# Seven products in place of eight for pairs of feed-forward column blocks, in a long float32 transformer kernel

## The reference

```
def swiglu(h, w_in, w_out):
    g, u = split_cols(h @ w_in, (D_FF, D_FF))        # D_FF = 2816
    return (jax.nn.silu(g) * u) @ w_out
x = x + 0.5 * swiglu(rms_norm(x, g), w_in[layer], w_out[layer])
```

## Time and profile before

| | |
|---|---|
| median of three runs | 1626.42 us (1625.85 to 1631.29) |
| profiled execution | 1626.7 us as the span from its first to its last instruction; the page gives no other time for it |
| PE busy | 1600.1 us (98%), 8058 matmuls |
| DVE busy | 1106.4 us (68%) |
| ACT busy | 862.0 us (53%) |
| POOL busy | 227.5 us (14%) |
| mean granted TensorE clock | 0.997 of full |

### The profile page before, as it was taken

One profiled execution on the slowest core, in us unless ns is written; L12 is line 12 of the kernel. 1 busy time (PEld: TensorE's weight loads), 2 busy tenths in 40 slices (PEclk: granted clock), 3 DMA queues, 4 the chain that ended last, 5 costly groups with the idle time before them and its releaser, 6 DMA issues.

```text
span 1626.7 us, 21211 instructions
## 1 busy us (share of the span) xinstructions
PE 1600.1 (98%) x8058; PEld 1337.7 (82%) x8058; DVE 1106.4 (68%) x1761; ACT 862.0 (53%) x1324; POOL 227.5 (14%) x351
## 2 busy tenths in 40 slices
PE   8999999999999999999999999999999999999998
PEld 6888877788888888888889888888889877888886
DVE  6775788867655556555596776655568997776566
ACT  5554556855545445444555555544454457454444
POOL 2499901000000000000000000000014442100000
PEclk9999999999999999999999999999999999999999
DMA  9766656445466565656655453565675554556653
GB/s 277 237 209 218 209 157 192 157 142 156 133 191 187 188 184 178 193 182 193 208 174 156 151 181 116 182 186 189 191 262 164 166 157 137 187 193 190 188 188 109
DMA packets 187543, 295.22 MB, mean 181 GB/s; under 512 B 13510, under 2 KB 108144, under 8 KB 186160
## 3 DMA queue, kind: packets, MB, share of 16 engines
q1 hardware_dynamic: 183264, 275.93, 54.6%
q0 software_dynamic: 3888, 17.60, 3.4%
q10 hardware_dynamic: 288, 0.33, 0.1%
HBM read 288.29 MB, written 5.25 MB: 180 GB/s over the span
## 4 chain that ended last, share of the span: by engine, by line
PE 86%; DVE 7%; ACT 3%; issue 2%; POOL 1%; DMA 0%; SPq 0%; DVEq 0%; ACTq 0%
PE b L445 25%; PE b L447 24%; PE b L446 24%; PE b L646 4%; DVE wlo L1655 2%; PE b L648 2%; ACT whi L1100 1%; PE b L669 1%; PE b L511 1%; PE b L899 1%; PE b L881 1%; PE b L608 1%; PE b L561 1%; PE b L527 1%; ACT R L1189 1%
## 5 line engine op out<-in xcount | busy, mean ns | idle before, releaser
L1655 DVE TENSOR_TENSOR wlo<-raw,whi 128x1024 fp32r<-128x1024 f32 (+1 forms) x523 | 648.5, 1243 | 436.5 <-ACT whi L1100 435.2
L1100 ACT ACTIVATE whi<-raw 128x1024 fp32r<-128x1024 f32 (+1 forms) x523 | 550.0, 1053 | 557.8 <-PE b L447 522.3
L445 PE MATMUL b<-whi,hT 128*128 128x512 f32 (+1 forms) x1040 | 413.4, 397 | 10.5 <-DVE wlo L1655 8.9
L447 PE MATMUL b<-whi,hT 128*128 128x512 f32 (+1 forms) x1040 | 405.1, 390 | 0.0
L446 PE MATMUL b<-wlo,hT 128*128 128x512 f32 (+1 forms) x1040 | 404.6, 389 | 0.0
L445 PE MATMUL b<-whi,oT 128*128 128x512 f32 x672 | 265.0, 394 | 0.0
L447 PE MATMUL b<-whi,oT 128*128 128x512 f32 x672 | 262.0, 390 | 0.0
L446 PE MATMUL b<-wlo,oT 128*128 128x512 f32 x672 | 261.6, 389 | 0.0
L445 PEld LDWEIGHTS b<-whi,hT 128*128 128x128 f32 x1040 | 196.1, 189 | 55.2 <-DVE wlo L1655 10.3
L447 PEld LDWEIGHTS b<-whi,hT 128*128 128x128 f32 x1040 | 196.0, 188 | 41.6
L446 PEld LDWEIGHTS b<-wlo,hT 128*128 128x128 f32 x1040 | 196.5, 189 | 37.9
(11 more groups left out here) (343 smaller groups left out, 1864.0 us busy)
## 6 DMA issues: line engine op xcount, KB each, us to landing
raw<-in_ffn_w_in SPq DMA_DIRECT2D x350, 256.0 KB, 3.2
raw<-in_ffn_w_out SPq DMA_DIRECT2D x88, 512.0 KB, 3.3
raw<-in_w_ff SPq DMA_DIRECT2D x64, 512.0 KB, 4.1
raw<-in_w_in SPq DMA_DIRECT2D x36, 512.0 KB, 3.7
raw<-in_x_w_kv SPq DMA_DIRECT2D x32, 512.0 KB, 4.1
raw<-in_even_w_in SPq DMA_DIRECT2D x24, 512.0 KB, 3.9
raw<-in_odd_w_in SPq DMA_DIRECT2D x24, 512.0 KB, 3.8
raw<-in_x_w_q SPq DMA_DIRECT2D x16, 512.0 KB, 4.0
```

What stands on the lines that cost most here:

```text
L445: T.matmul(out, ah, bh, start=start, stop=False, skip_group_check=skip)
L447: return T.matmul(out, al, bh, start=False, stop=stop, skip_group_check=skip)
L1100: E.activation(K.whi[j % NSPLIT][:, 0:n], K.raw[j % NRAW][:, 0:n], ACT.Copy).then_inc(*S.whi.done(j))
L1655: V.tensor_tensor(K.wlo[j % NSPLIT][:, 0:n], K.raw[j % NRAW][:, 0:n], K.whi[j % NSPLIT][:, 0:n].bitcast(F32), ALU.subtract).then_inc(*S.wl ...
```

## The change

For chunk pairs (2, 3), (4, 5) and (6, 7) of feed-forwards f1, f2 and f3, the product of h (256 x 1024) with a 1024 x 1024 part of `w_in` (512 gate and 512 up columns) is cut 2 x 2 and done with seven products of 128 x 512 by 512 x 512 in place of eight (`block`). Each product has two pieces of six matmuls each. A pair is called a block below, by its first chunk.

The seven need sums of the operands. POOL adds the sums of rows of h once for each feed-forward (2 operations of 128 x 1024 and 4 of 128 x 512) and makes four sums of weight tiles, T1 to T4, in two halves each, eight operations of 128 x 1024 for each block (`block_sums`). ACT and DVE split the sums as they split loaded tiles, so a block has 14 splits where two chunks had 8. Four partial results are joined on DVE out of PSUM and one copied by ACT; silus and multiplications are 128 x 512 now.

A block's eight tiles are loaded whole into buffers of their own (`tile_load`), 12 to 5 pieces ahead in SP's queue. These loads wait for POOL's sums that read the buffer before, in front of the ring's loads. The two or four rows of the chunks before come between the products: in block 2 behind P7 and P3, in blocks 4 and 6 behind P5, P2, P7 and P3. Chunk 8 has the four rows of chunks 6 and 7. The splits of the memory for layer 2 (`mem_halves(1, k)` and its low parts) move from chunks 5 and 6 of f1 to chunks 9 and 10 of f2.

```
+        self.tile = [R1[:, 1024 * i:1024 * i + 1024] for i in range(8)]
+        self.tsum = [R2[:, 1024 * i:1024 * i + 1024] for i in range(4)]
         self.vsb = sb("vsb", [P, 2, 512])
+        turned_heads = sb("sqj", [P, 1024])
+        self.tile += [self.vsb[:, :, :].rearrange("p a n -> p (a n)"), turned_heads[:, :]]
...
+    def factor(self, name, kt):
+        if name in ("P1", "P2", "P4"):
+            k, t = kt + 4 * (name != "P1"), int(name == "P4")
+            return tuple(a[:, k, P * t:P * t + P] for a in self.hT)
+        at = 512 * ("P5", "P6", "P7", "P3").index(name) + P * kt
+        return tuple(a[:, :, :].rearrange("p k t -> p (k t)")[:, at:at + P] for a in self.mT)
...
+    def ahead_of(self, c):
+        return [] if c == 0 else [c - 2, c - 1] if c - 2 in self.blocks else [c - 1]
 def downs(f, c):
     last = f.nch - 1
     if f.gated and c >= last - 1:
-        return [(last - 2, [c - last + 1])]
-    return [(c - 1, list(range(f.per)))] if 0 < c < last else []
+        more = [p for p in f.ahead_of(c) if p < last - 2] if c == last - 1 else []
+        return [(p, list(range(f.per))) for p in more] + [(last - 2, [c - last + 1])]
+    return [(p, list(range(f.per))) for p in f.ahead_of(c)] if c < last else []
+PRODUCTS = (("P1", 4, 1, "B11"), ("P6", 5, 1, "T2"), ("P5", 6, 1, "T1"), ("P2", 4, 0, "B21"), ("P7", 5, 0, "T3"),
+            ("P3", 6, 0, "B22"), ("P4", 5, 0, "T4"))
+TILES = {"B11": 0, "B12": 2, "B22": 4, "B21": 6}
+TSUMS = {"T1": 0, "T2": 2, "T3": 0, "T4": 2}
+TILE_LEAD = 12
...
-    Ffn("f1", 32, 0, "ffn2_w_in", "ffn2_w_out", 2816, True, 0.5, "x0"),
-    Ffn("f2", 40, 1, "ffn1_w_in", "ffn1_w_out", 2816, True, 0.5, "f1"),
-    Ffn("f3", 72, 1, "ffn2_w_in", "ffn2_w_out", 2816, True, 0.5, "x1"),
+    Ffn("f1", 32, 0, "ffn2_w_in", "ffn2_w_out", 2816, True, 0.5, "x0", (2, 4, 6)),
+    Ffn("f2", 40, 1, "ffn1_w_in", "ffn1_w_out", 2816, True, 0.5, "f1", (2, 4, 6)),
+    Ffn("f3", 72, 1, "ffn2_w_in", "ffn2_w_out", 2816, True, 0.5, "x1", (2, 4, 6)),
...
+            key, b, last_row = (f.name, c), f"{f.name}b{c}", [(p, kk) for p in f.ahead_of(c) for kk in range(f.per)]
+            shares = [0] * 7
+            for i in range(len(last_row)):
+                shares[5 - i % 4 if len(last_row) > 2 else 5 - i] += 1
+            for q, (name, bank, opens, of) in enumerate(PRODUCTS):
+                if name == "P2":
+                    pe.wait_ge(*S.snapped.at(key))
+                elif name == "P7":
+                    pe.wait_ge(*S.joined.at((*key, "U2")))
+                elif name == "P3":
+                    pe.wait_ge(*S.joined.at((*key, "V")))
+                elif name == "P4":
+                    pe.wait_ge(*S.joined.at((*key, "G1")))
+                else:
+                    open_bank(bank)
+                if name == "P6":
+                    pe.wait_ge(*S.slo.at((f.name, 1)))
+                for h in range(2):
+                    j = len(K.plan)
+                    K.at[b, 2 * q + h] = j
+                    kind = "tile" if of[0] == "B" else "sum"
+                    K.source.append((kind, key, f.slot(c, TILES[of] + h) if kind == "tile" else TSUMS[of] + h))
+                    K.plan.append((of, h, 0, 2, ((0, 512),)))
+                    pe.wait_ge(*S.wlo.at(j))
+                    hi, lo = K.split_views(j)
+                    for kk in range(2):
+                        ins = products(banks[bank][:, :], K.factor(name, 2 * h + kk), (hi[:, kk, :], lo[:, kk, :]),
+                                       bool(opens) and h == kk == 0, h == kk == 1, True)
+                    ins.then_inc(*S.dense.done(("w", j), *([(*key, name)] if h else [])))
+                    if q == 0 and h < len(f.ahead_of(c)):
+                        turn(f.ahead_of(c)[h])
+                for _ in range(shares[q]):
+                    p, kk = last_row.pop(0)
+                    down(p, [kk])
+            free[4] = (S.product.at((f.name, c, 0)),)
+            free[5] = (S.joined.at((*key, "U1")),)
+            free[6] = (S.joined.at((*key, "G0")),)
...
+            kind, of, i = K.source[j]
+            if kind == "ring":
+                act.wait_ge(*S.loaded[of % NRAW].at(j))
+            elif kind == "tile":
+                act.wait_ge(*S.tiled[i].at(of))
+            else:
+                act.wait_ge(*S.summed_w.at((*of, K.plan[j][0], K.plan[j][1])))
...
+            for o, p in enumerate(f.ahead_of(c)):
+                behind(o)
+                high(p)
+            behind(1)
+            act.wait_ge(*S.dense.at((*key, "P1")))
+            act.wait_ge(*S.product.at((f.name, c - 1, 1)))
+            E.activation(K.fs[0], banks[4][:, :], ACT.Copy).then_inc(*S.snapped.done(key))
+            behind(9)
+            opened(1, "G1")
+            behind(11)
+            opened(0, "G0")
+            weights(K.at[b, 13] + AHEAD)
...
+        def row_sums(i):
+            at = slice(1024 * i, 1024 * i + 1024)
+            act.wait_ge(*S.summed_w.at((f.name, "S", i)))
+            E.activation(K.mT[0][:, :, :].rearrange("p k t -> p (k t)")[:, at], K.R2[:, 2048 + 1024 * i:3072 + 1024 * i],
+                         ACT.Copy).then_inc(*S.shi.done((f.name, i)))
...
-    ffn(FFNS[1], {(5 + k // 4, k % 4): mem_halves(1, k) for k in range(8)}, {}, "f2", 40)
-    ffn(FFNS[2])
+    ffn(FFNS[1], {}, {}, "f2", 40)
+    ffn(FFNS[2], {(9 + k // 4, k % 4): mem_halves(1, k) for k in range(8)})
...
+            def joined(name, product, bank, first, out):
+                dve.wait_ge(*S.dense.at((*key, product)))
+                V.tensor_tensor(out, banks[bank][:, :], first, ALU.add).then_inc(*S.joined.done((*key, name)))
+            def gated(t, up):
+                dve.wait_ge(*S.silu.at((f.name, c, t)))
+                V.scalar_tensor_tensor(out=K.fa[(2 * c + t) % 4], in0=up, scalar=y[:, t:t + 1], in1=K.fs[2 - t],
+                                       op0=ALU.mult, op1=ALU.mult).then_inc(*S.product.done((f.name, c, t), (f.name, c + 1, t)))
+            for o, p in enumerate(f.ahead_of(c)):
+                reached(o + 1)
+                low(p)
+            reached(3)
+            dve.wait_ge(*S.snapped.at(key))
+            joined("U2", "P6", 5, K.fs[0], K.fs[2])
+            reached(5)
+            joined("V", "P5", 6, K.fs[0], K.fs[1])
+            reached(9)
+            dve.wait_ge(*S.joined.at((*key, "V")))
+            joined("G1", "P7", 5, K.fs[1], K.fs[1])
+            reached(11)
+            dve.wait_ge(*S.joined.at((*key, "U2")))
+            joined("G0", "P3", 6, K.fs[2], K.fs[2])
+            reached(12)
+            dve.wait_ge(*S.dense.at((*key, "P2")))
+            gated(0, banks[4][:, :])
+            reached(13)
+            joined("U1", "P4", 5, K.fs[0], K.fs[0])
+            dve.wait_ge(*S.joined.latest())
+            gated(1, K.fs[0])
...
+    def block_sums(f):
+        def then(name, i, out, a, b, op):
+            E.tensor_tensor(out, a, b, op).then_inc(*S.summed_w.done((f.name, name, i)))
+        def before_w():
+            pool.wait_ge(*S.summed_w.latest())
+        pool.wait_ge(*S.xlo.at(("h", f.name, 3, 1)))
+        A, rows = K.R2[:, 0:2048], K.R2[:, 2048:4096].rearrange("p (s k n) -> p s k n", s=4, k=4)
+        A4 = A.rearrange("p (k n) -> p k n", k=8)
+        for i in range(2):
+            hi, lo = (a[:, 4 * i:4 * i + 4, :].rearrange("p k t -> p (k t)").bitcast(F32) for a in K.hT)
+            then("A", i, A[:, 1024 * i:1024 * i + 1024], hi, lo, ALU.add)
+        A11, A12, A21, A22 = (A4[:, 4 * k:4 * k + 4, P * m:P * m + P] for m in range(2) for k in range(2))
+        before_w()
+        then("S1", 0, rows[:, 0, :, :], A21, A22, ALU.add)
+        then("S3", 0, rows[:, 2, :, :], A11, A21, ALU.subtract)
+        before_w()
+        then("S", 0, rows[:, 1, :, :], rows[:, 0, :, :], A11, ALU.subtract)
+        before_w()
+        then("S", 1, rows[:, 3, :, :], A12, rows[:, 1, :, :], ALU.subtract)
+        for n, c in enumerate(f.blocks):
+            key, b, old = (f.name, c), f"{f.name}b{c}", f"{f.name}b{f.blocks[n - 1]}"
+            def sum_tiles(name, h, old_b, old_o, out, a, b_tile, op, *tiles):
+                for i in tiles:
+                    pool.wait_ge(*S.tiled[f.slot(c, i)].at(key))
+                if old_o is not None:
+                    pool.wait_ge(*S.wlo.at(K.at[old_b, old_o]))
+                before_w()
+                E.tensor_tensor(out, a, b_tile, op).then_inc(*S.summed_w.done((*key, name, h)))
+            t, x = K.tsum, [K.tile[f.slot(c, i)] for i in range(8)]
+            for h in range(2):
+                sum_tiles("T1", h, old, 8 + h if n else None, t[h], x[2 + h], x[h], ALU.subtract, h, 2 + h)
+            if not n:
+                pool.wait_ge(*S.slo.at((f.name, 1)))
+            for h in range(2):
+                sum_tiles("T2", h, old, 12 + h if n else None, t[2 + h], x[4 + h], t[h], ALU.subtract, 4 + h)
+            for h in range(2):
+                sum_tiles("T3", h, b, 4 + h, t[h], x[4 + h], x[2 + h], ALU.subtract)
```

(85 more changed lines are left out.)

50 lines of the change are left out of this document (36 added, 14 removed).

## The result

The changed kernel takes 1761.2 us (median of four runs, 1758.0 to 1764.1) against 1626.3 for the kernel before on the same chip: 1.082 times as long, 95% interval 1.0805 to 1.0844. It is slower by 135 us where 113 were forecast, inside the range of 1655 to 1785. The profiled execution has a span of 1756.7 us, 130 more than before, and what follows accounts for these 130.

The account below looks back on a forecast made before the run. The prediction took PE, busy 98% of the span, to bound the kernel. Its three terms, (27.7 + 8.6 + 1.5) x 3 = 113 us, on the profiled 1626.7 us gave 1740, so 1739 for the median, range 1655 to 1785.

Parts of the forecast that it names:

- the saving: On PE, 84 matmuls in place of 96: 2.73 us less for a block, 24.6 us for nine.
- Taking turns: On the SBUF port: each POOL sum of 1024 columns keeps DVE from splitting for 2.27 us; 69% with full clock, 1739.
- Term 1: Blocks 2, 4 and 6 of each feed-forward: 123.1 us in place of 95.4, +27.7 us.
- Term 2: Start of each feed-forward: POOL's sums get between the root's short DVE operations, +8.6 us, bounds 0 and 11.
- Term 3: Chunk 8 of each feed-forward: its second matmul group waits for bank 5, +1.5 us, bounds 0.5 and 2.5.
- What I put at nothing: Tile loads hold back row loads, covered by DVE's delay; uncovered, about 6 us in block 2, 2.5 in block 4.
- the engines share: Rival, 11%: DVE's splits keep 1.23 us beside POOL's long sums; 7.5 us for each feed-forward, 1649.
- The clock's rival: 10%: PE, idle a quarter of the blocks, falls to 1.2 GHz for five of ten rows; 41 us more, 1780.
- That the gain arrives: Rival, 7%: POOL's sums hold DVE under about 0.4 us, so PE's saving shows; 1602 to 1618.
- The late transposes: PE's transposes wait for the multiplication in the blocks: 2.3 us, twice in each feed-forward.
- The marks: DVE's splits 1.7 us and more, POOL's sums 3.3 and more, f2's root 12, PE's idle time in blocks some 36.

Follow-up runs that it names:

- x6_few_lead5: The changed kernel with POOL's sums cut to four columns and TILE_LEAD 5 in place of 12: 1622.8 us, ratio 0.9973 to the kernel before.

## Why the prediction was right, step by step

**What bounds the kernel, and the saving: right.** PE does 108 matmuls less at 0.227 us. The saving is real, but no more than 4 us of it reached the end in any run, even with sums for nothing.

**Taking turns: right, shown.** 80 us of the 135 vanish when POOL only writes, and the splits go back from 2.0 us to 1.22. The length of a sum, 2.42 us by extension from 256 and 512 columns, was measured at 2.40.

**Term 1, the blocks, +27.7 us: right.** In f2, from block 2's first matmul at 709.42 to the end of block 6's P4 at 830.75, the trace has 121.3 us for 123.1 forecast: +25.9. The parts agree less well than the sum. From PE's first matmul of block 2 to the start of its P4, from there to block 4's, and from there to the end of block 6's it was 34.3, 43.3 and 43.7 us, for 33.0, 44.1 and 46.0. Block 2 was taken too short and block 6 too long, since PE runs without waits for splits from 812.9 on.

**Term 2, the start, +8.6 us: the mechanism right, the size too small.** From f2's first matmul to the first one behind chunk 0's transposes it was 623.30 to 638.66, and is 667.07 to 693.20: 10.8 us more, at the end of its bounds. Then the lower clock costs one piece of 12 matmuls 0.2 us each, 2.4 us, which no term had. The multiplication slips by 11.5 us against PE's first matmul (13.16 us behind it before, 24.65 now), where I had 10.7. Of the 2.1 us of slack that I took off, 1.3 were there, since the transposes start 15.0 us behind the first matmul before and 25.2 now, 10.2 later. The last 0.6 of the 10.8 is the transposes themselves at the lower clock.

**Term 3, chunk 8, +1.5 us: right in kind.** PE waits 0.7 us for bank 4 and 0.9 for bank 5 there, and its pieces then run without a gap; about 1.8 us in all, from 830.75 to the transposes at 835.24.

**What I put at nothing.** The rows' loads were covered, as said. The tile loads' wait in front of f1 and f3 was not seen: it holds the cross attention's loads and costs 4.9 us in the trace. Without it the feed-forwards cost 42.7, 41.4 and 43.8 us, where I had 37.8. Of the 3.6 us of difference in f2, the lower clock is 2.4, the start 2.2 and chunk 8 0.3, and the blocks take 1.8 back; 0.5 stay open. The three and the 4.9 make 132.8. The profiled execution is 130.0 us longer, since PE was 1.9 us ahead of the kernel before already in front of f1, and gains 0.9 behind f3, in work that the change leaves alone.

**The rivals.** That the engines share is excluded by the splits' lengths. The clock's rival was half seen: the clock falls behind the 10 us wait at the start and in single windows of the blocks (0.83 in 750 to 760 us, 0.87 in 800 to 810), but not through half of their rows. About a dozen of the 372 matmuls of f2's blocks are some 0.43 us apart, 2.4 us where the rival had 13.7 in a feed-forward; the clock's mean over the kernel is 0.978. That the gain arrives is excluded by the result, and by x6_few_lead5 even for sums that hold DVE for next to nothing. The late transposes, which the sharing rival priced at 2.3 us twice in a feed-forward, cost that only while POOL takes turns (13.8 us in six waits); in x6_few_lead5 it is 4.5 us in six.

**The marks.** Splits at 1.7 us and more: 2.0. Sums at 3.3 and more: wrong, 2.85 us in the mean of f2's blocks. Many meet no split and keep 2.40, as the one at 759.93, which starts beside a join. The root at 12 us: 13.0. PE's idle time in blocks, 36 us: by distances between starts PE takes 34.5 us more than the 86.8 of its own work in f2's three. The waits put 19.1 of it down to splits, 4.6 to the multiplications and nothing to loads; the rest does not show as waits, since a matmul's recorded duration covers part of each gap, and the lower clock is in it.

## What to carry to other kernels

Before moving work to an idle engine, ask which port its operands come through: here POOL was idle 86% of the time, and its sums still stood in DVE's queue, at 2.3 us apiece by the estimate that came out, because DVE's splits and the sums both read two operands from SBUF. Saving matmuls by the seven products halved the time behind which each split can hide (pieces of 6 matmuls for 12) while a block has 14 splits for 8; count the other engines' work per matmul first. And when one delay is taken away, look for what it covered: the rows' held loads cost nothing in the change and some 31 us once the sums were short.

## What the runs showed of the hardware that was not expected

POOL's sums get their turn between two dependent DVE operations on one or two columns, so a chain of 17 of them went from 2.7 to 13 us. After ten microseconds in which PE had no matmuls its granted clock was 0.50, and the first 12 matmuls behind the wait took 0.43 us each. Behind the shorter waits of 9 us (sums after the root) and 7 us (sums by DVE) the clock fell too, to means of 0.58 and 0.66 over the ten microseconds that hold the wait, and behind the 6.0 us wait of the run with short sums 12 matmuls were 0.43 us apart.
